# A two-unit expert body with one uniform inner loop, on one Trainium2 core

## The reference, cut to what matters

```python
def moe_swiglu(h, w_router, b_router, w_gu, w_down):
    logits = (h @ w_router).astype(jnp.float32) + b_router.astype(jnp.float32)
    top_logit, top_idx = lax.top_k(logits, TOP_K)
    top_w = jax.nn.softmax(top_logit, axis=-1)
    ...
    for e in range(N_EXPERTS):
        out = out + gates[..., e:e + 1] * swiglu(h, w_gu[e], w_down[e])
```

## Time and profile before

| | before |
|---|---|
| median of 3 runs | 1477.02 us (1476.58 to 1481.11) |
| the profiled execution | 1480.24 us, span 1478.5 us |
| PE busy | 1441.5 us, 98% of the span |
| PE weight loads busy | 1310.0 us, 89% |
| DVE, ACT, POOL busy | 399.3, 337.9, 38.5 us |
| mean DMA rate over the span | 306 GB/s |
| instruction packets (queue q8) | 106, 1.74 MB |

### The profile page before, as it was taken

One profiled execution on the slowest core, in us unless ns is written; L12 is line 12 of the kernel. 1 busy time (PEld: TensorE's weight loads), 2 busy tenths in 40 slices (PEclk: granted clock), 3 DMA queues, 4 the chain that ended last, 5 costly groups with the idle time before them and its releaser, 6 DMA issues.

```text
span 1478.5 us, 44860 instructions
## 1 busy us (share of the span) xinstructions
PE 1441.5 (98%) x19512; PEld 1310.0 (89%) x19515; DVE 399.3 (27%) x697; ACT 337.9 (23%) x570; POOL 38.5 (3%) x60
## 2 busy tenths in 40 slices
PE   9999999999999999999899899899989989999988
PEld 6888888888888999999799799899989989999986
DVE  7976454577874000000000000000000000000045
ACT  7565444375433001000000000100010000010032
POOL 1010000000000000000000000000000000000000
PEclk9999999999999999999999999999999999999999
DMA  8577555456137999999899899989989989999980
GB/s 316 183 248 237 193 171 196 173 196 232 59 130 252 377 391 381 380 392 363 313 408 368 296 400 384 372 320 393 373 320 391 376 308 394 389 360 408 410 347 29
DMA packets 124377, 451.96 MB, mean 306 GB/s; under 512 B 14000, under 2 KB 14000, under 8 KB 124256
## 3 DMA queue, kind: packets, MB, share of 16 engines
q1 hardware_dynamic: 119952, 435.21, 78.7%
q0 software_dynamic: 4160, 14.85, 2.9%
q10 hardware_dynamic: 144, 0.03, 0.0%
HBM read 442.71 MB, written 7.34 MB: 304 GB/s over the span
## 4 chain that ended last, share of the span: by engine, by line
PE 96%; issue 2%; DVE 1%; DMA 1%; ACT 0%; POOL 0%; POOLq 0%; DVEq 0%; ACTq 0%
PE PS L961 49%; PE PS L959 12%; PE PS L524 10%; PE PS L526 9%; PE PS L525 9%; PE PS L988 2%; PE PS L575 1%; DMA SC<-in_ple_w_gate 1%; PE PS L819 0%; PE PS L665 0%; PE PS L1071 0%; PE PS L943 0%; PE PS L593 0%; PE PS L929 0%; PE PS L909 0%
## 5 line engine op out<-in xcount | busy, mean ns | idle before, releaser
L961 PE MATMUL PS<-raw,gain 128*32 128x384 f32 x2712 | 325.3, 490 | 0.0
L961 PE MATMUL PS<-SC,gain 128*32 128x384 f32 x2664 | 322.3, 501 | 0.0
L959 PE MATMUL PS<-SC,gain 128*32 128x128 f32 x2664 | 309.5, 277 | 0.0
L959 PE MATMUL PS<-raw,gain 128*32 128x128 f32 x2712 | 306.6, 273 | 0.0
L959 PEld LDWEIGHTS PS<-SC,gain 128*32 128x32 f32 x2664 | 291.9, 112 | 12.0 <-issue 8.7
L959 PEld LDWEIGHTS PS<-raw,gain 128*32 128x32 f32 x2712 | 295.0, 110 | 1.7 <-issue 1.4
L2001 DVE TENSOR_TENSOR junk<-junk,PS 128x384 f32<-128x384 f32 x56 | 31.0, 554 | 808.0 <-ACT junk L1393 795.3
L524 PE MATMUL PS<-w_hi,xT_hi 128*128 128x512 f32 x536 | 213.6, 398 | 0.8 <-DVE w_lo L1504 0.5
L526 PE MATMUL PS<-w_lo,xT_hi 128*128 128x512 f32 x536 | 209.1, 390 | 0.0
L525 PE MATMUL PS<-w_hi,xT_lo 128*128 128x512 f32 x536 | 208.9, 390 | 0.0
L961 PEld LDWEIGHTS PS<-raw,gain 128*32 128x32 f32 x2712 | 207.3, 108 | 0.1
(11 more groups left out here) (299 smaller groups left out, 1163.4 us busy)
## 6 DMA issues: line engine op xcount, KB each, us to landing
raw<-in_e_w_gu SPq DMA_DIRECT2D x226, 512.0 KB, 7.3
SC<-in_e_w_gu SPq DMA_DIRECT2D x222, 512.0 KB, 6.0
SC<-in_e_w_down SPq DMA_DIRECT2D x114, 512.0 KB, 7.2
raw<-in_e_w_down SPq DMA_DIRECT2D x110, 512.0 KB
raw<-in_ffn_w_gu SPq DMA_DIRECT2D x44, 512.0 KB, 4.9
raw<-in_w_in_c SPq DMA_DIRECT2D x32, 512.0 KB, 4.9
raw<-in_ffn_w_down SPq DMA_DIRECT2D x22, 512.0 KB, 4.6
raw<-in_w_in_ab SPq DMA_DIRECT2D x20, 512.0 KB, 7.3
```

The source lines that it names most:

```text
L959: pe.matmul(PS[CAP:P, bank, k * P:(k + 1) * P], tokens[k], w[:, MAIN:N], start=start and k == 0, stop=stop, skip_group_check=True)
L961: m = pe.matmul(PS[32 * k:32 * (k + 1), bank, 0:MAIN], tokens[k], w[:, 0:MAIN], start=start, stop=stop, skip_group_check=True)
```

## The change

The item body on PE goes from four units of code to two. The first unit keeps its own code, because `turn_rows` and the start of a new sum lie in it; all others, the next item's unit 0 among them, run in one loop (u = 1 to 6, in the last item 1 to 5). For that:

- the turn of the next item's unit 0 moves from the start of the item to the end of the last loop pass (the same place in PE's order); item 0 keeps its first turn ahead;
- `turn_xg` moves from behind the pass u = 4 to ahead of the loop, directly behind the turn of unit 1;
- the waits for `xe`, once per item, become waits of every loop pass for two new counters, `go_act` and `go_dve`, which ACT and DVE raise once per unit: with the copy of `xe` where there is one, else with an increment of their own;
- every down product closes its sum (`stop`), which changes no instruction count;
- ACT's wait for `rows_written` moves from the unit u = 5 to ahead of the next item's output copy;
- `turn_rows` makes each of its four products in three column groups of 32, so twelve.

The number of strip products, transposes, element-wise operations and transfers of weights per item is as before. The core of the diff:

```diff
@@ turn_rows
-                        m = pe.matmul(PS[0:CAP, 3, 0:2], sel16[:, t, 0:CAP], pick[:, t, a, :], start=(t == 0 and a == 0),
-                                      stop=(t == T - 1 and a == 1), skip_group_check=True)
+                        for c in range(0, CAP, 32):
+                            m = pe.matmul(PS[c:c + 32, 3, 0:2], sel16[:, t, c:c + 32], pick[:, t, a, :],
+                                          start=(t == 0 and a == 0), stop=(t == T - 1 and a == 1), skip_group_check=True)
@@ PE, item
                 if first:
                     pe.wait_ge(silu_done, FB + 1)
-                    unit_gu(G_MOE + 4, 0, None, (0,))
-                unit_turn(i * EU + (FB + 1))
-                if not first:
-                    unit_gu(G_MOE + 4, i * EU, None, (0,))
+                    unit_gu(G_MOE + 4, 0, (0,))
+                    unit_turn(FB + 1)
+                else:
+                    unit_gu(G_MOE + 4, i * EU, (0,))
...
                 unit_turn(i * EU + (FB + 2))
-                def unit(u):
-                    unit_gu(G_MOE + 4, i * EU + u)
-                    unit_down(G_MOE + 8, i * EU + u + (FB + 1), False, i * EU + u)
-                    unit_turn(i * EU + u + (FB + 2))
-
-                with pe.Fori(1, EU - 2) as u:
-                    unit(u)
                 if not last:
                     turn_xg(i + 1)
-                unit(EU - 2)
+
+                with pe.Fori(1, EU - 1 if last else EU) as u:
+                    pe.wait_ge(go_act, i * EU + u)
+                    pe.wait_ge(go_dve, i * EU + u)
+                    unit_gu(G_MOE + 4, i * EU + u)
+                    unit_down(G_MOE + 8, i * EU + u + (FB + 1), i * EU + u)
+                    unit_turn(i * EU + u + (FB + 2))
                 if last:
...
-                else:
-                    unit_gu(G_MOE + ITEM - 2, i * EU, i + 3)
-                    unit_down(G_MOE + ITEM + 2, i * EU + (FB + EU), True, i * EU)
@@ ACT, xg and item
-                m.then_inc(xg_act, 1)
+                m.then_inc(go_act, 1)
...
                 unit_silu()
+                if not first:
+                    act.sem_inc(go_act, 1)
+                    act.wait_ge(rows_written, i * 16)
                 output(G_MOE + 4, i * EU)
...
                     if end:
                         xg(i + 2)
-                        act.wait_ge(rows_written, i * 16 + 16)
+                    else:
+                        act.sem_inc(go_act, 1)
                     unit_hT(i * EU + u + (FB + 2))
@@ DVE, xg and item
-                m.then_inc(xg_ready, 1)
+                m.then_inc(go_dve, 1)
...
                     if end:
                         xg(i + 2)
+                    else:
+                        dve.sem_inc(go_dve, 1)
+                    if end:
                         dve.wait_ge(rows_held, i + 1)
...
                 if not last:
                     unit_hidden(i * EU + EU + (FB + 1))
+                    dve.sem_inc(go_dve, 1)
```

## The result

The changed kernel takes 1441.53 us (median of four runs, 1439.88 to 1442.24), the kernel before 1477.74 us beside it (1476.58 to 1481.11): a ratio of 0.975 (0.9731 to 0.9769). The forecast was 1446 us with a range of 1439 to 1456. So the likeliest case came about, and the time lies 4.5 us under its value.

A forecast was written before the change was run, and what follows sets the result against it. PE, busy 98% of the span, was taken as the bound, stalled by code fetched anew at each item-loop jump. 1480.24 - 33.3 + 1.5 - 0.6 = 1447.8 us on the profiled execution, taken as 1446 us; range 1439 to 1456.

The forecast's parts named there:

- the likeliest case: The shorter item body on PE is held, so the jump stalls go: 1446 us, chance 0.84.
- Part 1, the jump: At PE's item-loop branch, five stalls and the low clock behind them go: 33.3 us less.
- nearer to 2.7 than to 11: Reason for pricing the new body's jump, up to 5.6 packets, like the unit loop's (2.7), not the old body's (11).
- The packets: On code queue q8, some 50 packets fewer: 5 turns of 11, less what the shorter code saves.
- Part 2, the row fetch: Ahead of the earlier row transposes, one wait of 0.1 to 1.5 us in item 0, none later; 1.5 taken.
- Part 3, the row products: Twelve column-group products at 0.5 us per execution, eight executions: 0.6 us less in all.
- the "free" end of the bounds: Lower bound for the row products over eight executions, if they cost nothing: -4.6 us.
- Part 4: Two more PE waits in each of 47 unit passes cost 0, at most 0.1 us a pass, 4.7 us.
- the weights: SP's weight stream keeps up without the stalls, as in item 1 at 380 GB/s: cost 0.
- Not held: Rival: the new item body is not held either, all five jumps stay, 1478 us; chance 0.08.
- The row fetch late in every item: Rival: PE waits 1.5 us on the row fetch in each of six items more, 1455 us; chance 0.04.
- The two waits: Rival: the new waits hold PE's sequencer at each loop head, 1 us a pass, 1493 us; chance 0.04.

The follow-up runs named there:

- 1,444 records: Changed kernel with 120 tiny products of zeros padded into the looped item body ahead of the unit loop: 1464.4 us, one run.
- the wait taken away: Changed kernel with DVE's cast of the row numbers ahead of the table work in item 0: 1440.69 us, ratio 0.9737; again beside the changed kernel, 1442.91 us.
- the kernel that does this part alone: Kernel before with only the row products put in three column groups of 32: 1474.02 us, ratio 0.9966.
- a body of three units: Changed kernel with pass u = 6 written out behind the unit loop in all items but the last: 1469.53 us, ratio 0.9932.
- 250 pads: Changed kernel with 250 tiny products of zeros in the looped item body ahead of the unit loop, 1,704 records: 1557.14 us, one run.
- the hint: Kernel before, four units kept, with a branch prefetch hint at the top of each turn of PE's item loop: 1451.57 us, ratio 0.9809.

## Why the prediction came out as it did

**Part 1, the jump: right.** The branch at 213 ns (forecast 250), no wait ahead of the turn in items 2 to 6, clock 1.00 in each. The size of 33.3 us, taken from the stages and not from the 22.9 us of waiting, was the right one: items 2 to 6 now last as long as item 1 (116.96 to 117.07 us), so the whole difference is gone. Had the sum gone by the list of waits, it would have been 10.4 us short, the share of the clock. The choice that rested on the thinnest ground was the price of a loop of 5 to 6 packets between 3 (free) and 11 (6.67 us). It held, but "nearer to 2.7 than to 11" was no sound reason: the price of the branch is a step between 1,444 and 1,704 records, and nothing in the rows said on which side of it 1,204 lies. As far as the rows go, that choice was luck. The step lies between 6.1 and 8.0 packets, by the 214 to 236 records of a packet in the earlier trace rows. The packets of the earlier trace rows proved that something is held; how much, only a loop of another length could show.

The Trainium skill (Runtime: NRT & Kernel Launch, Instruction fetch mechanics) gives PE 128 KiB, or 2,048 instructions, in blocks of 16 KiB. The runs agree if one of its eight blocks is filled ahead, which no run shows by itself; they show no more than the two sizes between which the step lies. Its sentence that only two blocks are kept, by which this change would have gained nothing, is against the runs: with 1,444 records in the loop 41 packets came in the whole kernel, one more than with 1,204.

**The packets: right in kind, low in number.** "Some 50 fewer" were 66: five turns of 11 are 55, and the shorter text, with two units less in three copies of the item, is taken to be the rest.

**Part 2, the row fetch: right on the trace, without weight in the time.** One wait of 1.4 us in item 0, none later; item 0 took 1.57 us longer, forecast 1.5. Over the runs of the kernels with this order the wait was 0.4 to 2.7 us. But with the wait taken away the time did not fall measurably. What was forecast as 1.5 us on the path is smaller than what the clock in the end stretch varies by.

**Part 3, the row products: the term that was mis-sized.** Forecast -0.6 us in all, measured 0.46 to 0.55 us in each of items 1 to 6 and 0.35 ahead of item 0. In item 0 itself it is only 0.1: there the row products follow the turn, not a strip, and the kernel before has no idle 0.44 us ahead of them (its trace has that gap seven times, where the prediction counted eight). That makes some -3.6 us, and -4.7 by the medians of the kernel that does this part alone, about the "free" end of the bounds, -4.6. PE and its weight loads around the new row products of item 1, to be read against the earlier trace rows:

```profile
595.57 0.49 PE L963 MATMUL PS<-SC,gain 128*32 128x384 f32 x1
595.58 0.48 PE L954 MATMUL PS<-seg,SC 128*32 128x2 bf16 x9
595.90 0.30 PE L961 MATMUL PS<-raw,gain 128*32 128x128 f32 x1
595.92 0.21 PE L954 MATMUL PS<-seg,SC 128*32 128x2 bf16 x3
```

```profile
595.57 0.42 PEld L954 LDWEIGHTS PS<-seg,SC 128*32 128x32 bf16 x8
```

From the last strip to the next it is 0.33 us in place of 0.69. The idle 0.44 us is gone, and the twelve products overlap the strips beside them: 0.22 us in all behind the step of 0.11, where the prediction had priced each at the step of a strip, 0.055 us and 0.66 for twelve. That step is a mean over products of 128 and 384 columns, and these have two. The 0.36 us seen here is most of the gain of an item; where the other 0.1 to 0.2 us comes from was not followed up. Of the 4.5 us by which the forecast was high this is about 3; the rest is within what the end stretch varies by, as is the 2.6 us that the profiled executions differ by there.

**Part 4 and the weights: right.** The new waits cost nothing, even four times over. The stream kept up: 380 to 387 GB/s in items 1 to 6 with PE busy throughout and no wait on weights in its list.

**The rivals.** Not held: refuted here, but it is exactly what a body of three units or 250 pads does. The row fetch late in every item: no such wait. The two waits: no gap at any pass.

**What stays open.** Why the clock falls after PE's wait for DVE in the end stretch in one execution and not in another. In the profiled kernels with wide row products item 7 with the end takes 150.3 to 150.9 us (153.7 with the hint, 2.8 us of issue wait among it), in those with column groups 146.4 to 150.3 us; whether the one has to do with the other was not tried.

## What to carry to other kernels

Where an engine waits and the profile names "issue", look at its sequencer's branch times and at the packets of its code queue, and compare the stages on either side, since the granted clock adds to the wait (here 10.4 us on 22.9). A loop whose body is held jumps in 0.2 us, one that is not pays some 6 us and the clock behind it, in a step: one long loop body of PE is worth shortening until the queue of packets falls silent, and a branch prefetch hint gives most of it (27 of 33 us here) with one line, at the price of a wait where the loop is left (2.8 us here). Small products placed among strips should use the strips' own column groups.

## What the runs showed of the hardware that was not expected

- The prefetch hint hides a jump of 6 us almost wholly, though all the code is still fetched (102 packets, branch 476 ns).
- The branch's time hardly depends on how far the body is over the limit: 5,950, 5,876 and 5,935 ns for 1,704, 1,786 and 2,352 records. What an item loses in all does vary: 8.2 to 9.3, 5.8 to 6.1 and 5.4 to 7.6 us.
- The granted clock fell behind small products in a row (of zeros, 8 columns) although PE had not been idle: behind 120 of them, 3.1 us, two of the six items show some 3.4 us at 1.2 GHz with PE busy throughout, the other four none. With 250 it fell within the pads of item 1, ahead of the wait on "issue" of 2.1 us there, and every item from 1 to 6 runs at a mean of 0.94 to 0.96 (0.969 over the span). Which property of the products does it was not tried.
